# Spread rows issued by GpSimd alone, and a pair's convolution placed behind both units of the next pair

## What is computed

```python
def conformer_conv(h, w1, b1, dw, dwb, ln_g, ln_b, w2, b2):
    u = h @ w1 + b1
    a, g = jnp.split(u, 2, axis=-1)
    u = a * jax.nn.sigmoid(g)
    u = dwconv(u, dw) + dwb
    u = jax.nn.silu(layernorm(u, ln_g, ln_b))
    return u @ w2 + b2
```

```python
mod_l = (silu_c @ mod_w[i] + mod_b[i]).reshape(b, N_MOD, 1, D_MODEL)
```

## Time and profile before

| what | value |
|---|---|
| median of 3 runs | 3192.09 us (3188.49 to 3193.14) |
| the profiled execution's own time | 3197.25 us |
| its span | 3195.2 us |
| PE busy | 3009.5 us (94%) |
| DVE, ACT, POOL busy | 48%, 37%, 7% |
| mean granted TensorE clock | 0.975 of full speed |
| convolution module from its first product to its last convolution | 1566.7 to about 1797.2 us of the span |

### The profile page before, as it was taken

How to read it: one execution, slowest core, us unless ns; L and a number is a source line. 1 busy time by engine, 2 the same in 40 slices (tenths; PEclk the granted TensorE clock), 3 DMA queues, 4 the chain that set the end, 5 groups by cost and what they waited for, 6 DMA issues and landing times.

```text
span 3195.2 us, 42092 instructions
## 1 busy us (share of the span) xinstructions
PE 3009.5 (94%) x17944; PEld 2504.1 (78%) x17944; DVE 1545.7 (48%) x2477; ACT 1195.9 (37%) x1939; POOL 237.0 (7%) x326
## 2 busy tenths in 40 slices
PE   8998999989999989999968799999999999998898
PEld 7987898879977757888644378887787888787898
DVE  6664554655545545444411354443545444444565
ACT  5443443654444434222311343232324232333443
POOL 0000000000012210000110000000000000143100
PEclk9999999999999999999989899999999999999999
DMA  7555666656654443232364533333323323266353
GB/s 229 186 166 182 220 229 220 196 198 226 215 146 85 75 125 119 92 106 93 114 194 122 168 115 129 119 119 119 119 93 108 103 93 105 68 122 98 109 185 132
DMA packets 348314, 450.77 MB, mean 141 GB/s; under 512 B 10816, under 2 KB 330592, under 8 KB 335840
## 3 DMA queue, kind: packets, MB, share of 16 engines
q1 hardware_dynamic: 341488, 431.61, 41.2%
q0 software_dynamic: 6480, 15.89, 5.3%
q10 hardware_dynamic: 160, 0.59, 0.1%
HBM read 437.63 MB, written 1.05 MB: 137 GB/s over the span
## 4 chain that ended last, share of the span: by engine, by line
PE 85%; DVE 7%; ACT 4%; DMA 3%; issue 1%; SPq 0%; POOL 0%; DVEq 0%; ACTq 0%; POOLq 0%
PE ps L1056 25%; PE ps L1058 24%; PE ps L1057 24%; PE ps L1237 2%; PE ps L1098 2%; DMA raw<-in_mod_w 1%; PE ps L1077 1%; PE ps L1079 1%; PE ps L1078 1%; DVE lo L1549 1%; PE ps L1228 1%; DVE lo L1552 1%; ACT hi L1270 1%; PE ps L1089 1%; PE ps L1137 1%; PE ps L1216 1%
## 5 line engine op out<-in xcount | busy, mean ns | idle before, releaser
L1056 PE MATMUL ps<-XN,hi 128*128 128x256 f32 (+1 forms) x3008 | 1021.5, 340 | 46.2 <-DVE XN L1575 20.9
L1057 PE MATMUL ps<-XN,hi 128*128 128x256 f32 (+1 forms) x3008 | 1003.3, 334 | 0.0
L1058 PE MATMUL ps<-XN,lo 128*128 128x256 f32 (+1 forms) x3008 | 1002.9, 333 | 0.0
L1056 PEld LDWEIGHTS ps<-XN,hi 128*128 128x128 f32 x3008 | 579.4, 193 | 162.9 <-DVE XN L1575 35.4
L1549 DVE TENSOR_TENSOR lo<-raw,hi 128x1024 fp32r<-128x1024 f32 (+1 forms) x313 | 386.7, 1235 | 516.7 <-ACT hi L1270 504.5
L1058 PEld LDWEIGHTS ps<-XN,lo 128*128 128x128 f32 x3008 | 578.9, 192 | 54.6
L1057 PEld LDWEIGHTS ps<-XN,hi 128*128 128x128 f32 x3008 | 580.0, 193 | 51.2
L1270 ACT ACTIVATE hi<-raw 128x1024 fp32r<-128x1024 f32 (+1 forms) x313 | 326.4, 1043 | 513.7 <-PE ps L1058 429.6
L1552 DVE TENSOR_TENSOR lo<-raw,hi 128x1024 fp32r<-128x1024 f32 (+1 forms) x313 | 380.9, 1217 | 0.0
L1056 PE MATMUL ps<-H,hi 128*128 128x512 f32 (+1 forms) x1024 | 371.3, 363 | 0.0
L1057 PE MATMUL ps<-H,hi 128*128 128x512 f32 (+1 forms) x1024 | 371.2, 363 | 0.0
(11 more groups left out here) (231 smaller groups left out, 3275.0 us busy)
## 6 DMA issues: line engine op xcount, KB each, us to landing
raw<-in_mlp_w SPq DMA_DIRECT2D x128, 1024.0 KB, 5.3
raw<-in_mod_w SPq DMA_DIRECT2D x96, 1024.0 KB, 4.9
raw<-in_ffn_w_in SPq DMA_DIRECT2D x44, 1024.0 KB, 5.6
raw<-in_attn_w_in SPq DMA_DIRECT2D x36, 1024.0 KB, 5.3
raw<-in_na_wqkv SPq DMA_DIRECT2D x24, 1024.0 KB, 5.3
raw<-in_ffn_w_out SPq DMA_DIRECT2D x16, 1024.0 KB, 5.4
raw<-in_mlstm_w_in SPq DMA_DIRECT2D x12, 1024.0 KB, 5.4
raw<-in_cv_w SPq DMA_DIRECT2D x12, 1024.0 KB, 7.2
```

What stands on the lines that cost most here:

```text
L1056: e.matmul(out, whi, xhi, start=first, stop=False)
L1057: e.matmul(out, whi, xlo, start=False, stop=False)
L1058: i = e.matmul(out, wlo, xhi, start=False, stop=last)
```

## The change

In each round of `conformer` the two convolutions of pair c - 1 are placed behind A(c) instead of between G(c) and A(c). All 16 spread DMAs of each pair are issued by GpSimd, on one semaphore per `UX` buffer; SP issues none, and its step `cv_spread` is gone. The waits of TensorE and VectorE for the spread name the new semaphore. Nothing else is different: the same products, DMAs and bytes.

```diff
--- before.py
+++ after.py
@@ -147,7 +147,7 @@
 
     m.ps = [ctx.enter_context(nc.psum_tensor(f"ps{i}", [P, 512], F32)) for i in range(8)]
     m.sem = {n: ctx.enter_context(nc.semaphore(f"s_{n}"))
-             for n in ["acc", "act", "high", "dve", "low", "pool", "ld", "x0", "x1", "taps", "uxs0", "uxs1", "uxp0", "uxp1", "pv", "ci", "pos", "cst", "tb0", "tb1", "out"]
+             for n in ["acc", "act", "high", "dve", "low", "pool", "ld", "x0", "x1", "taps", "ux0", "ux1", "pv", "ci", "pos", "cst", "tb0", "tb1", "out"]
              + [f"raw{i}" for i in range(RAW)]}
     m.lay = lay
     return m
@@ -795,13 +795,13 @@
         def evac_a(t, b, u):
             p.do("cv_a", 2 * c + t, t, b, u)
             if t == 1:
-                p.do("cv_spread", c, 3 if c < 3 else 2)
+                p.do("cv_spread", c)
 
         p.linear("cv_w1_2", 0, 0, KT, 1024 + c * 256, 256, x, evac_g, outer=c == 0)
+        p.linear("cv_w1_2", 0, 0, KT, c * 256, 256, x, evac_a)
         for k in (2 * c - 2, 2 * c - 1):
             if k >= 0:
                 convolve(k)
-        p.linear("cv_w1_2", 0, 0, KT, c * 256, 256, x, evac_a)
     p.pace = p.credit = 0.0
     for k in (KT - 2, KT - 1):
         p.mod_unit()
@@ -1000,13 +1000,6 @@
     return 0, (kt + 1) // 2 * cols, kt * cols
 
 
-def spread(e, m, c, g, signal, name):
-
-    for i in range(4):
-        e.dma_start(m.UX[32 * i:32 * i + 32, c % 2, g, :, 0:572],
-                    m.U[32 * g:32 * g + 32, 2 * (c % 2):2 * (c % 2) + 2, i:i + 572]).then_inc(*signal.says((name, c)))
-
-
 def sync(e, w, m, p, T, sig):
     def begin():
         for i in range(2):
@@ -1025,11 +1018,6 @@
                     T[src][layer][k0:k0 + kt * P, c0:c0 + cols].rearrange("(k p) n -> p k n", p=P)).then_inc(
             *sig[f"raw{j % RAW}"].says(("raw", j)))
 
-    def cv_spread(c, g0):
-        w.wait_ge(("cv_u", 2 * c + 1), ("conv", 2 * c - 3) if c >= 2 else None)
-        for g in range(g0, 4):
-            spread(e, m, c, g, sig[f"uxs{c % 2}"], "ux_sp")
-
     def finish(s):
         for half in range(2):
             at = half * KT // 2
@@ -1038,7 +1026,7 @@
                 *sig["out"].says(("stored", half)))
         w.wait_ge(("stored", 1))
 
-    go_through(p, {"begin": begin, "load": load, "cv_spread": cv_spread, "finish": finish})
+    go_through(p, {"begin": begin, "load": load, "finish": finish})
 
 
 def tensor(e, w, m, p, acc):
@@ -1230,7 +1218,7 @@
         f.then_inc(*acc.says(("acc", b, u), ("na_mixed", layer, i), ("na_group", layer, group)))
 
     def cv_conv(k, b, u):
-        w.wait_ge(("ux_sp", k // 2), ("ux_pool", k // 2), ("wd", k), free_of(b, u))
+        w.wait_ge(("ux", k // 2), ("wd", k), free_of(b, u))
         for j in range(8):
             for g in range(4):
                 rows = m.UX[:, k // 2 % 2, g, k % 2, :].rearrange("p (s t) -> p s t", s=2)
@@ -1842,9 +1830,7 @@
                         ALU.subtract).then_inc(*dve.says(("free", b, u), ("ob", layer, tile) if last else None))
 
     def cv_a(k, t, b, u):
-        w.wait_ge(("acc", b, u), ("cv_s", k), "cv_pads")
-        if k >= 4:
-            w.wait_ge(("ux_sp", k // 2 - 2), ("ux_pool", k // 2 - 2))
+        w.wait_ge(("acc", b, u), ("cv_s", k), "cv_pads", ("ux", k // 2 - 2) if k >= 4 else None)
         e.scalar_tensor_tensor(
             out=m.U[:, k % 4, :].rearrange("p (s t) -> p s t", s=2)[:, :, 15:271],
             in0=m.ps[b].rearrange("p (s t) -> p s t", s=2), scalar=param(m, "cv_b1_2", k),
@@ -1978,10 +1964,14 @@
         for a, b in ((0, 15), (271, 288)):
             e.memset(m.U.rearrange("p b (s t) -> p (b s) t", s=2)[:, :, a:b], 0.0).then_inc(*pool.says("cv_pads"))
 
-    def cv_spread(c, g0):
+    def cv_spread(c):
+
         w.wait_ge(("cv_u", 2 * c + 1), ("conv", 2 * c - 3) if c >= 2 else None)
-        for g in range(g0):
-            spread(e, m, c, g, sig[f"uxp{c % 2}"], "ux_pool")
+        for g in range(4):
+            for i in range(4):
+                e.dma_start(m.UX[32 * i:32 * i + 32, c % 2, g, :, 0:572],
+                            m.U[32 * g:32 * g + 32, 2 * (c % 2):2 * (c % 2) + 2, i:i + 572]).then_inc(
+                    *sig[f"ux{c % 2}"].says(("ux", c)))
 
     def sc_pads(s):
         w.wait_ge(("xn", s, KT - 1))
```

## The result

The changed kernel takes 3154.3 us (median of 4 runs, 3149.68 to 3159.94); the kernel before, run again beside it, 3190.29 us (4 runs). The ratio is 0.9888, with a 95% interval of 0.9867 to 0.9909: about 1.1% or 36 us faster. Forecast were 3141 us, in a range of 3133 to 3160. The direction came out and SP's wait went as forecast, but the time is 13 us above the forecast, and of the forecast gain of 51 us 15 are missing (51.2 against 36.0). The profiled execution took 3159.94 us (span 3157.9) against 3197.25 before.

What follows compares the result with a forecast made beforehand. TensorE bounds the kernel, with 53.8 us of waits for `mod_w_2` and `UX` in the convolution module. Gains of 46.4 + 3.3 + 3.0 - 1.5 = 51.2 us take the median from 3192.09 to 3140.9 us, range 3133 to 3160.

Steps and rivals of the forecast that it cites:

- SP's wait: Pairs ahead of G(1), G(2), G(3): second load no longer held in SP's queue, each pair costs 1.7 us; 46.4 us gained.
- the sum's own bounds: Forecast time between 3136 us (last spread at +12.2, loads in time, both clocks full) and 3147 us.
- the first rival: Loads beside a spread get almost no DMA engine time; waits move ahead of A(c+1): 3164 us, chance 0.13 including 3184 form.
- the signs named: Convolution module: listed limits on waits, SP and GpSimd issue times, gate-unit times and module length that would show the forecast right.
- the slow tail: Three gate units behind the gaps, slowed by a low clock, return to 11.1 us plus fold work: 3.3 us gained.
- The rule of the Trainium skill: Issuing from another engine saves only issue time, three times 2.53 us of SP: 3184.5 us; chance 0.13 shared with the first rival.
- The last spread: At tile 6: spread lands +15 us after release, TensorE waits 8.4 us instead of 11.2; 3.0 us gained, between 5.8 and -0.7.
- The collision of loads: Pairs ahead of A(1), A(2), A(3): loads meet the spread and may land late; -1.5 us charged for all three.
- The sum: Gains of 46.4, 3.3 and 3.0 less 1.5 make 51.2 us, taking the median to 3140.9 us.
- What I had costed at nothing: Low halves, spreads of pairs 0 to 2, ScalarE's later evictions and GpSimd's further issues, behind VectorE's later tables: hidden, cost 0.
- The slower rival: GpSimd's software queue takes longer per DMA with sixteen than 0.53 us; at 3 us each, 3232 us; chance 0.03.

Runs made afterwards that it cites:

- Runs 1 and 5: 1: kernel before with only the convolutions moved behind A(c), 3177.53 us; 5: Run 4's kernel with spreads issued by GpSimd and SP as before, 3152.27 us.
- Run 2: Whole change with the convolutions put back between G(c) and A(c), GpSimd alone issuing the spreads: 3190.86 us, ratio 0.9995 to the kernel before.
- run 3: Whole change, with SP holding the third modulation load behind A(3) and all later ones until the last spread has landed: 3150.26 us.
- Run 4: Whole change, with VectorE writing both U tiles of a pair before both WD tables, which wait for the convolutions: 3131.35 us.

## Why the prediction was right, and where it fell short

The forecast of 3141 us was 13 us too low. 3154.3 lies outside the sum's own bounds (3136 to 3147) and inside the stated range (3133 to 3160) only because that was widened toward the first rival, whose mechanism did appear. Of the signs named, SP's issues 0.9 us apart, G(1) in 11.6 us and GpSimd's sixteen in 8.5 us came; the waits for `mod_w_2` (3.2 and 3.3 us against at most 3), the wait at tile 6 (15.5 against 6 to 12) and the module (194.9 against 175 to 184) did not. (The 1797.2 that I had taken for the end of the last convolution is the end of the sum behind it; the convolution ends at 1795.2.)

**SP's wait (46.4 us) and the slow tail (3.3 us): right.** The pairs ahead of G(1), G(2) and G(3) have no wait, and G(1) runs at full clock. Runs 1 and 5 show that the load had been held by its place behind SP's wait and not by the DMA engines alone. The rule of the Trainium skill that I weighed against this ("DMA: Bandwidth & Descriptors", section on issuing engines not being separate DMA queues: another issuer only saves issue time) gave 3184.5 and did not describe the whole change. Run 2, which changes the issuer alone, gained nothing, as the rule has it, but not for its reason: the 42.6 us of waits for the loads went, and 54.0 us of waits for `UX` came.

**The last spread (+3.0 us): mis-sized.** I put the landing at +15 us after the release, between +12.2 and +18.7; it was +22.1. The wait is 15.5 us and not 8.4, a loss of 7.1 against the forecast. The step that failed was the upper bound: I took the slowest landing of a single `UX` DMA (10.7 us) from a spread that only twelve software DMAs and four of SP's shared with loads. Here the two loads left at 1720.99 and 1721.85, 5.8 and 6.7 us after the release, and the sixteenth DMA then took 13.8 us. Without them it is +13.6 (run 3), below the +15 I chose.

**The collision of loads (-1.5 us): mis-sized.** The pairs ahead of A(2) and A(3) take 6.2 and 6.3 us instead of 1.7, and the value units behind them 11.7 and 13.0 us instead of 11.1, at clocks of 0.94 and 0.85: 37.2 against 25.6, or 11.6 us. Of these, 6.5 are the two waits; the other 5.1 are the same matmuls at the lower clock, for which this term had nothing, although the gate units before had shown such a tail. I had bounded the second load of a pair by 11.6 + 3 = 14.6 us; these took 15.2 and 15.8, so the bound was short by up to 1.2 us. What failed above all is the step from it to -1.5 for all three, which leaned to no wait because SP's four DMAs no longer stood ahead of the load. I had looked for the collision ahead of A(1), where the loads start with the spread. There the second load took 11.6 us and was in place (1602.28) within 1 us of its use:

```profile
raw<-in_mod_w SPq DMA_DIRECT2D x1, 1024.0 KB, 11.6
```

Where the spread has a lead of 6 us, for which I had called the bound no worse, the load takes 4 us more and comes too late. This is the first rival's mechanism: with the last spread, 17.2 of the 22.5 us that I had put on it, though none of it ahead of A(1), where I had placed the largest wait.

**The sum.** 51.2 - 7.1 - 10.1 = 34.0 us against 33.7 measured in the module.

**What I had costed at nothing.** The low halves, the tables and the sum in `SA` were indeed hidden: TensorE waits for none of them longer than before. But the clause that VectorE's table of tile 2c holds back `U` of tile 2c + 1, and with it the spread, had a price I saw only for the last pair: it starts the spreads of pairs 1 and 2 just ahead of the pair loads, too. Run 4, which only takes this wait out of the way, removes both losses: 23 us in the medians (25 by the ratios to the kernel before, 0.9888 and 0.9809), 28.9 in the module (194.87 - 166.00).

The slower rival did not come: GpSimd needs 8.5 us for sixteen DMAs, as for twelve in proportion. The D of that rival, the time of a whole spread, did reach 22 us in the change and 20 to 26 in run 2, which is why a cover of one gate unit (run 2) is not enough while a whole round is.

## What to carry to other kernels

A queue that works in order makes everything behind a wait as late as what is waited for: look for a transfer that could have left long ago, behind one that waits for another engine, and give the waiting kind a queue that has nothing else to do. Then ask what the freed transfers will meet, and release the competing burst as early as its data allows; here one VectorE instruction that waits for a convolution, placed ahead of the data that the burst needed, cost 23 us, more than half of what the change had won. Take the time of a burst beside other loads from the sum of both, not from the slowest row of another mix of transfers.

## What was not expected of the hardware

In this module transfers beside each other cost about their sum. Sixteen spread DMAs (2.3 MB) took 13.6 us by themselves; two modulation loads take 7.5 us by themselves (4.8 for one and 2.7 more for the one behind it); together 21.1, and 22.1 were measured. Beside the second spread of the change went three loads, the third sent at 1633.27 and in place 15.7 us later, 24.5 us after the spread's first DMA; the same sum gives 13.6 + 4.8 + 2 x 2.7 = 23.8. In run 2, with further loads behind, a spread took 20 to 26 us. A load took 4.8 us alone and 15.2 to 15.8 us as the second of a pair that joined a running spread after 6 us. The Trainium skill says in "DMA: Bandwidth & Descriptors", section "Queues, rings and completion order", that each DMA engine serves the queues that have work for it in turn, a packet at a time. That both kinds of transfer finish late agrees with it, but no run here changes the sizes of packets, so how much each gets per turn stays open.
